# The first level of a chunk inverse, untransposed copy: products X + X Ts in place of transposes

## The chip, the cores and the metric

The kernel runs on one core of a Trainium2 chip. The metric is device time in microseconds for one execution: one layer of a hybrid block (an RWKV-7 recurrence in 8 heads beside sliding-window attention in 8 heads, then a SwiGLU feed-forward layer) for 1024 tokens of width 1024, in float32.

## What is computed

```python
def step(S, inp):                       # one token of the RWKV-7 recurrence, per head
    r_t, w_t, k_t, v_t, kk_t, a_t = inp
    sa = jnp.einsum('bhvk,bhk->bhv', S, -kk_t)
    S = (S * w_t[:, :, None, :]
         + sa[..., None] * (kk_t * a_t)[:, :, None, :]
         + v_t[..., None] * k_t[:, :, None, :])
    return S, jnp.einsum('bhvk,bhk->bhv', S, r_t)
...
o_rwkv = rwkv7_time_mix(p_rwkv, ...)
o_attn = swa_sink_attention(q, k_att, v_att, sinks[l])
x = x + jnp.concatenate([o_rwkv, o_attn], axis=-1) @ w_out[l]
h = rmsnorm(x, norm_ffn_g[l])
gate, up = jnp.split(h @ w_gate_up[l], 2, axis=-1)
x = x + (jax.nn.silu(gate) * up) @ w_down[l]
```

The kernel does not step through tokens. It takes the 1024 tokens in 8 tiles of 128, and within a tile the dependence of a token on the tokens before it is a triangular system with unit diagonal, one 128x128 matrix per head. Its inverse is what this case is about.

## The kernel before

The program has seven stages, one after another on each engine: the input projection, its lanes, attention, the recurrence (the functions named `stage5_...`), the output projection, the feed-forward layer and the last norm. Each engine has its own function per stage, and the functions wait for each other with semaphores. The order on every engine is the order in which the code is written; nothing reorders it.

**The recurrence.** `stage5_tensor` (TensorE), `stage5_vector` (VectorE), `stage5_scalar` (ScalarE), `stage5_sync` (DMA queue) and `stage5_gpsimd` each loop over t = 0 to 7, the tiles of 128 tokens. The 8 heads are worked in two groups g of four, since four 128x128 results fill one PSUM bank of 128x512. `Plan` gives every job (a name, a group, a tile) its bank: `C.claim` waits until the bank's last reader is done, `C.done` marks the last matmul, `C.result` waits for that mark, `C.read` frees the bank after the read, and `C.emptied` waits until that read has ended.

**The inverse of one tile.** VectorE inverts the 16x16 diagonal blocks (`lanes`), and two DMAs bring them as `XT` (the inverse, transposed) into SBUF. Two levels then double the block size, 16 to 32 (level 1) and 32 to 64 (level 2). A level needs both the inverse so far, `X`, and its transpose, `XT`:

- `corners(n, t)`, line 1359: TensorE forms NB times X in the banks `tn0`, `tn1`. VectorE masks the result to the level's corner blocks into `Ts1` or `Ts2` (line 1556).
- `updates(n, t)`, line 1366: TensorE forms Ts times XT in the banks `yn0`, `yn1`, and VectorE adds the changed half of it to `XT` (line 1563), freeing the bank.
- `transposed("x1", g, t)`: after level 1, TensorE waits until the add of group g has ended, transposes its four blocks of the new `XT` (line 1358) into the bank `x10` or `x11`, and ScalarE copies the bank to `X` (`keep_x`, line 1497). Level 2 needs this `X`. At the start of a tile `transposed("xa", ...)` and `keep_x("xa", ...)` do the same with the `XT` that the DMA brought.

**What stands around it.** Between level 1 and level 2 TensorE has two further pieces: `outputs(t - 1)` (line 1385), four transposes of the tile before, from t = 1 on, and `cumulative(pe, t + 2)` (line 1213), eight recorded matmuls for the tile after the next, up to t = 5. On VectorE `normalise(t - 1)` (line 1619) stands behind level 1's mask, and `outputs(t - 1)` (lines 1625 and 1629) behind level 1's adds. In the last tile VectorE also has `mix_low(0)` (line 1266), which prepares the output projection, between `outputs` and level 2's mask. `prepare` (lines 1251 to 1257) and `lanes(t + 1)` follow level 2's adds.

Of the kernel before, what the change touches and what calls it, by code (L numbers as in the profile page):

```python
# [7 lines left out]
ALU = mybir.AluOpType  # L8
# [73 lines left out]
def hybrid_block(nc, x_t, par_in, w_in, w0, w_up, a_up, g_up, sinks, w_out, w_gate_up, w_down, norm_final_g,  # L82
# [10 lines left out]
    def at(name, kb, shape, dt=F32):  # L93
        return nc.alloc_sbuf_tensor_at(name, shape, dt, offset=BASE + int(kb * K))
# [8 lines left out]
    with root:  # L103
# [133 lines left out]
        X, XT = at("X", 112, [P, H, P]), at("XT", 116, [P, H, P])  # L237
# [14 lines left out]
        x1 = at("x1", 72, [P, KD, T])  # L252
# [150 lines left out]
        def row(ap):  # L403
            return ap.rearrange("p a n -> p (a n)")
# [445 lines left out]
        for t in range(-1, NT):  # L850
            n = t + 1
# [331 lines left out]
        C = Plan(order5 + [("ot", NT - 1, 7)])  # L1183
# [47 lines left out]
        def exponentials(act, t, *js):  # L1231
            for j in js:
                b = C.result(act, f"cum{j}", t)
                if t:
                    act.wait_ge(s_prep, 4 * t)
                v = b[:, 0:2 * (P + 1)].rearrange("p (a n) -> p a n", a=2)
                c = slice(2 * j, 2 * j + 2)
                act.activation(ein[:, c, :], v[:, :, :], ACT.Exp, scale=-DECAY)
                act.activation(ecs[:, t, c] if t else ecs0[:, c], v[:, :, P], ACT.Exp, scale=-DECAY)
                if t:  # L1240
                    act.activation(ems[:, t, c], v[:, :, 0], ACT.Exp, scale=DECAY)
                ins = act.activation((einv if t else einv0)[:, c, :], v[:, :, 1:P + 1], ACT.Exp, scale=DECAY)
                C.read(ins, f"cum{j}", t)
# [15 lines left out]
        def mix_high(act, n):  # L1259
            k = MIX_ORDER[n]  # L1260
            act.activation(mhi[:, k, :], mix[:, k, :], ACT.Copy).then_inc(s_m, 1)
# [86 lines left out]
        def stage5_tensor(pe):  # L1348
            def four(b, g, lhs, rhs):
                for j in range(4):  # L1350
                    mm = pe.matmul(b[:, j * P:(j + 1) * P], lhs(4 * g + j), rhs(4 * g + j), start=j == 0, stop=j == 3,  # L1351
                                   skip_group_check=True)
                return mm

            def transposed(job, g, t):
                b = C.claim(pe, f"{job}{g}", t)
                for j in range(4):
                    mm = pe.transpose(b[:, j * P:(j + 1) * P], XT[:, 4 * g + j, :], ident)  # L1358
                C.done(mm, f"{job}{g}", t)
# [7 lines left out]
            def updates(n, t):  # L1367
                m = Ts1 if n == 1 else Ts2
                for g in range(2):
                    C.emptied(pe, f"t{n}{g}", t)  # L1370
                    b = C.claim(pe, f"y{n}{g}", t)
                    C.done(four(b, g, lambda h: m[:, h, :], lambda h: XT[:, h, :]), f"y{n}{g}", t)

            def tokens(t):
                for kind, m in (("bt", ab), ("kt", kT)):
                    b = C.claim(pe, kind, t)
                    for p in range(NP):
                        mm = pe.transpose(b[:, p * P:(p + 1) * P], m[:, p, tok(t)], ident)
                    C.done(mm, kind, t)
# [20 lines left out]
            for t in range(NT):  # L1400
# [4 lines left out]
                for g in range(4):  # L1405
                    C.emptied(pe, f"b{g}", t)
                corners(1, t)
                updates(1, t)
                if t:
                    outputs(t - 1)  # L1410
                for g in range(2):
                    C.emptied(pe, f"y1{g}", t)
                    transposed("x1", g, t)
                if t + 2 < NT:
                    cumulative(pe, t + 2)
                corners(2, t)
                updates(2, t)

                if t:
# [35 lines left out]
                if more:  # L1455
                    b = C.claim(pe, "S", t)
# [35 lines left out]
        def stage5_scalar(act):  # L1492
            low, high = slice(0, HD), slice(HD, P)

            def keep(job, t, dst, rows=slice(0, P)):
                b = C.result(act, job, t)
                C.read(act.activation(dst, b[rows, :], ACT.Copy), job, t)

            def keep_x(job, t):
                for g in range(2):  # L1500
                    keep(f"{job}{g}", t, row(X[:, 4 * g:4 * g + 4, :]))

            def tokens(t):
                keep("bt", t, bt[:, :])
                keep("kt", t, kt_[:, :])

            exponentials(act, 1, 0, 1)
            tokens(0)
            for t in range(NT):
                last = t == NT - 1  # L1510
                keep_x("xa", t)
                if last:
                    mix_high(act, 0)
                keep_x("x1", t)
                if last:
                    mix_high(act, 1)
                if t + 2 < NT:
                    exponentials(act, t + 2, 0, 1)
                if last:
                    mix_high(act, 2)  # L1520
                act.wait_ge(s_r, t + 1)
                act.activation(rs_[low, :], bank[0][low, :], ACT.Copy).then_inc(s_rlow, 1)
                act.wait_ge(s_u, t + 1)
                act.activation(us_[low, :], bank[2][low, :], ACT.Copy).then_inc(s_ulow, 1)
                keep("R", t, rs_[high, :], high)
                keep("U", t, us_[high, :], high)
                if last:
                    mix_high(act, 3)
                if last:
                    for s in range(2):  # L1530
                        OUT.split_hi(act, s, 0, first=True)
                else:
                    C.emptied(act, "S", t)
                    act.wait_ge(s_fac, t + 1)
                    for p in range(NP):
                        ins = act.activation(S[:, p, :], Sn[:, p, :], ACT.Copy, scale=facs[:, t + 1, p:p + 1])
                    ins.then_inc(s_S, 1)
                act.wait_ge(s_oc, t + 1)
                act.activation(osq[:, :, :], oc[:, :, :], ACT.Square).then_inc(s_osq, 1)
                if t + 1 < NT - 1:  # L1540
                    tokens(t + 1)

        def stage5_vector(dve):
            order = Order(dve, "rec_order")

            def halves(ap, n, second):

                w = BLK << (n - 1)
                return ap.rearrange("p h (b n) -> p h b n", n=2 * w)[:, :, :, w * second:w * second + w]
# [9 lines left out]
            def updates(n, t):  # L1559
                for g in range(2):  # L1560
                    b = C.result(dve, f"y{n}{g}", t).rearrange("p (h n) -> p h n", h=4)
                    v = halves(XT[:, 4 * g:4 * g + 4, :], n, 1)
                    C.read(dve.tensor_tensor(v, halves(b, n, 1), v, ALU.add), f"y{n}{g}", t)

            def lanes(t):
# [75 lines left out]
            for t in range(NT):  # L1641
# [22 lines left out]
                if not last:  # L1664
                    b = C.result(dve, "S", t)
# [9 lines left out]
                b = C.result(dve, "O", t)  # L1675
# [829 lines left out]
```

## Time and profile before

| | us |
|---|---|
| median of 3 runs | 1366.65 |
| lowest, highest of the 3 | 1365.69, 1497.57 |
| the profiled execution | 1372.2 |
| its span (first to last recorded instruction) | 1370.1 |
| recurrence, first transposes of t = 0 to the first product of the output projection | 364.65 to 587.82 |

The profile is of one execution. A row of the time line gives the start, the time that the instructions of that row took from the first start to the last end, the engine, the line of the code, the operation with output and inputs, the number of recorded instructions, and in brackets the idle time before it with what ended that idle time. A float32 matmul of the program stands in the trace as two recorded matmuls, a float32 transpose as one. The recorded end of a matmul is modelled and overlaps the next one, so the time that a group takes of TensorE is read from its start to the start of the next group. PE is TensorE, PEld its weight loads, DVE VectorE, ACT ScalarE.

### The profile page before, as it was taken

What the parts mean: (1) busy time and instruction counts of PE and PEld (TensorE: products, weight loads), DVE (VectorE), ACT (ScalarE), POOL (GpSimd) and SP (SyncE); (2) the same over time, 40 slices, a digit from 0 to 9 for tenths busy, and PEclk for the clock granted to TensorE, in tenths of its full rate; (3) what the DMA queues carried; (4) which work ended last, traced back from release to release, by engine and by line L of the source; (5) the groups of instructions that cost most, each with busy time, mean ns of one, the idle gap of its engine ahead of it and who ended that gap; (6) DMA issues with size and microseconds to landing.
All of it is one profiled execution on the core that took longest, in us unless ns stands there. A gap on an engine that the chain in (4) does not pass through costs nothing.

```text
span 1370.1 us, 18353 instructions
## 1 busy us (share of the span) xinstructions
PE 1322.4 (97%) x7169; PEld 1094.5 (80%) x7169; DVE 807.8 (59%) x1212; ACT 466.9 (34%) x864; POOL 169.1 (12%) x144
## 2 busy tenths in 40 slices
PE   7999999898899999999999999999999999999996
PEld 6888887555699899888878888888888887888885
DVE  6644422499677777554476565665656655454545
ACT  6111132577422332333453333333333333021232
POOL 0000000044300000000004223332233100000000
PEclk9999999999999999999999999999999999999999
DMA  5111132200212221333212232222321284241323
GB/s 211 55 46 46 35 104 93 70 1 17 60 52 53 82 66 46 118 128 113 80 64 77 93 92 92 65 75 93 93 93 58 74 298 155 77 154 46 110 91 138
DMA packets 68864, 120.34 MB, mean 88 GB/s; under 512 B 20912, under 2 KB 37296, under 8 KB 68528
## 3 DMA queue, kind: packets, MB, share of 16 engines
q1 hardware_dynamic: 68784, 119.23, 27.0%
q8 instruction: 55, 0.90, 0.3%
q14 instruction: 25, 0.20, 0.0%
HBM read 89.30 MB, written 29.36 MB: 87 GB/s over the span
## 4 chain that ended last, share of the span: by engine, by line
PE 86%; DVE 7%; DMA 2%; ACT 2%; issue 1%; SPq 0%; DVEq 0%; ACTq 0%
PE bank L344 29%; PE bank L2271 27%; PE bank L397 6%; PE bank L1351 4%; PE bank L1225 2%; PE bank L472 2%; PE bank L358 2%; PE bank L1477 1%; PE bank L1435 1%; PE bank L1429 1%; DMA land<-hid_scratch 1%; DVE st L1151 1%; DVE scores L1128 1%; DMA hid_scratch<-hid 1%; PE bank L1358 1%
## 5 line engine op out<-in xcount | busy, mean ns | idle before, releaser
L323 DVE TENSOR_TENSOR ring_wlo<-ring_raw,ring_whi 128x1024 fp32r<-128x1024 f32 (+1 forms) x62 | 73.8, 1190 | 241.1 <-ACT ring_whi L317 240.9
L317 ACT ACTIVATE ring_whi<-ring_raw 128x1024 fp32r<-128x1024 f32 (+1 forms) x62 | 63.7, 1030 | 308.4 <-PE bank L344 232.2
L2271 PE MATMUL bank<-thi,ahi 128*128 128x512 f32 x320 | 124.5, 389 | 0.0
L2271 PE MATMUL bank<-tlo,ahi 128*128 128x512 f32 x320 | 124.5, 389 | 0.0
L2271 PE MATMUL bank<-thi,alo 128*128 128x512 f32 x320 | 124.5, 389 | 0.0
L344 PE MATMUL bank<-hhi,ring_whi 128*128 128x512 f32 x288 | 115.0, 399 | 0.0
L344 PE MATMUL bank<-hlo,ring_whi 128*128 128x512 f32 x288 | 112.8, 392 | 0.0
L344 PE MATMUL bank<-hhi,ring_wlo 128*128 128x512 f32 x288 | 112.8, 392 | 0.0
L2271 PE MATMUL bank<-x1hi,ahi 128*128 128x512 f32 x240 | 93.4, 389 | 0.0
L2271 PE MATMUL bank<-x1lo,ahi 128*128 128x512 f32 x240 | 93.4, 389 | 0.0
L2271 PE MATMUL bank<-x1hi,alo 128*128 128x512 f32 x240 | 93.4, 389 | 0.0
L344 PE MATMUL bank<-x1hi,ring_whi 128*128 128x512 f32 x176 | 68.8, 391 | 1.7 <-DVE ring_wlo L323 1.7
L2271 PEld LDWEIGHTS bank<-thi,alo 128*128 128x128 f32 x320 | 60.1, 188 | 12.5
L2271 PEld LDWEIGHTS bank<-tlo,ahi 128*128 128x128 f32 x320 | 60.1, 188 | 12.5
L2271 PEld LDWEIGHTS bank<-thi,ahi 128*128 128x128 f32 x320 | 60.1, 188 | 12.4
L344 PE MATMUL bank<-mhi,ring_whi 128*128 128x512 f32 x168 | 66.0, 393 | 2.7 <-DVE gat L2225 2.7
L344 PE MATMUL bank<-x1lo,ring_whi 128*128 128x512 f32 x176 | 68.5, 389 | 0.0
L344 PE MATMUL bank<-x1hi,ring_wlo 128*128 128x512 f32 x176 | 68.5, 389 | 0.0
L344 PE MATMUL bank<-mlo,ring_whi 128*128 128x512 f32 x168 | 66.1, 393 | 0.0
L344 PE MATMUL bank<-mhi,ring_wlo 128*128 128x512 f32 x168 | 66.0, 393 | 0.0
L344 PEld LDWEIGHTS bank<-hhi,ring_whi 128*128 128x128 f32 x288 | 54.5, 189 | 12.0 <-issue 1.0
L344 PEld LDWEIGHTS bank<-hlo,ring_whi 128*128 128x128 f32 x288 | 54.4, 189 | 11.9 <-issue 1.0
(314 smaller groups left out, 2863.5 us busy)
## 6 DMA issues: line engine op xcount, KB each, us to landing
ring_raw<-in_w_down SPq DMA_DIRECT2D x24, 512.0 KB, 3.6
hid_scratch<-hid SPq DMA_DIRECT2D x22, 512.0 KB, 6.2
ring_raw<-in_w_in SPq DMA_DIRECT2D x20, 512.0 KB, 3.7
raw_a<-in_w_gate_up SPq DMA_DIRECT2D x20, 512.0 KB, 4.5
raw_b<-in_w_gate_up SPq DMA_DIRECT2D x20, 512.0 KB, 5.1
land<-hid_scratch SPq DMA_DIRECT2D x16, 512.0 KB, 4.1
xin<-in_x_t SPq DMA_DIRECT2D x8, 512.0 KB, 9.6
n_scratch<-NB SPq DMA_DIRECT2D x8, 512.0 KB, 3.2
```

The lines of the kernel that those rows point to most:

```text
L317: act.activation(self.ring.hi[:, s, 0:self.kt, :], self.ring.raw[:, s, 0:self.kt, :], ACT.Copy).then_inc(self.ring.hi_ready, 1)
L323: dve.tensor_tensor(self.ring.lo[:, s, 0:self.kt, :], self.ring.raw[:, s, 0:self.kt, :], self.ring.hi[:, s, 0:self.kt, :].bitcast(F32), AL ...
L344: mm = pe.matmul(o[:, :], wpart[:, s, k, :], apart[:, k, c], start=i == 0, stop=i == n - 1)
L358: mm = pe.matmul(bank[self.J.bank_of[f"{s}{half}"]][:, :], wpart[:, s, ks[n], :], apart[:, ks[n], c], start=n == 0 and i == 0, stop=n == l ...
L397: mm = pe.matmul(o[:, :], wpart[:, s, k, :], apart[:, k, c], start=k == 0 and i == 0, stop=k == self.kt - 1 and i == 2)
L472: mm = pe.matmul(b[:, :], wpart[:, s, k, :], apart[:, k, c], start=k == 0 and i == 0, stop=k == KD - 1 and i == 2)
L1128: ins = dve.scalar_tensor_tensor(sc[:, h0:h0 + 3:2, :], b[:, 0:2 * BAND].rearrange("p (a n) -> p a n", a=2), HD ** -0.5, bias[:, h0:h0 + 3 ...
L1151: order(dve.tensor_reduce(st8[:, 0, :], sc[:, :, :], AX_X, ALU.max))
L1225: mm = pe.matmul(b[e][:, i * 2 * P:(i + 1) * 2 * P].rearrange("p (a n) -> p a n", a=2), src[r, 2 * g + i, tok(t)], rho_alpha(t, r, 2 * g + ...
L1351: mm = pe.matmul(b[:, j * P:(j + 1) * P], lhs(4 * g + j), rhs(4 * g + j), start=j == 0, stop=j == 3, skip_group_check=True)
L1358: mm = pe.transpose(b[:, j * P:(j + 1) * P], XT[:, 4 * g + j, :], ident)
L2271: mm = pe.matmul(b[:, :], w[:, k, :], m[:, k, :], start=opens and k == 0 and i == 0, stop=not (j, n) in parts and k == 3 and i == 2, skip_ ...
```

## The change

Level 1 no longer transposes the updated `XT`. In `updates`, when n is 1, TensorE forms XT times Ts for the same four heads into the bank `x1g`, right behind the product for `y1g`; both use the `XT` from before the update. VectorE adds the changed half of that bank to `X`, ahead of its add to `XT`. The eight transposes of a tile at this place and ScalarE's two copies of a tile are gone. The waits of TensorE for `y10` and `y11` to be emptied stay where they were.

```diff
@@ stage5_tensor, updates
                     C.emptied(pe, f"t{n}{g}", t)
                     b = C.claim(pe, f"y{n}{g}", t)
                     C.done(four(b, g, lambda h: m[:, h, :], lambda h: XT[:, h, :]), f"y{n}{g}", t)
+                    if n == 1:
+                        b = C.claim(pe, f"x1{g}", t)
+                        C.done(four(b, g, lambda h: XT[:, h, :], lambda h: m[:, h, :]), f"x1{g}", t)
@@ stage5_tensor, the loop over t
                     outputs(t - 1)
                 for g in range(2):
                     C.emptied(pe, f"y1{g}", t)
-                    transposed("x1", g, t)
                 if t + 2 < NT:
                     cumulative(pe, t + 2)
                 corners(2, t)
@@ stage5_scalar
-                keep_x("x1", t)
@@ stage5_vector, updates
                     b = C.result(dve, f"y{n}{g}", t).rearrange("p (h n) -> p h n", h=4)
                     v = halves(XT[:, 4 * g:4 * g + 4, :], n, 1)
+                    if n == 1:
+                        bx = C.result(dve, f"x1{g}", t).rearrange("p (h n) -> p h n", h=4)
+                        u = halves(X[:, 4 * g:4 * g + 4, :], n, 0)
+                        C.read(dve.tensor_tensor(u, halves(bx, n, 0), u, ALU.add), f"x1{g}", t)
                     C.read(dve.tensor_tensor(v, halves(b, n, 1), v, ALU.add), f"y{n}{g}", t)
```

TensorE's order in one tile (t = 1), from the first transposes of `XT` to level 2's second product. A row is a group of equal instructions of the program, the number at its end how many. Before:

```order
L1358 MATMUL bank<-cst,XT 128x128 x8
L1351 MATMUL bank<-X,NB_89 128x128 x8
L1351 MATMUL bank<-XT,Ts_90 128x128 x8
L1385 MATMUL bank<-cst,on 128x128 x4
L1358 MATMUL bank<-cst,XT 128x128 x8
L1213 MATMUL bank<-cst,sgt 128x129 x4
L1351 MATMUL bank<-X,NB_89 128x128 x8
L1351 MATMUL bank<-XT,Ts_91 128x128 x8
```

And the same stretch of the changed kernel:

```order
L1358 MATMUL bank<-cst,XT 128x128 x8
L1351 MATMUL bank<-X,NB_89 128x128 x8
L1351 MATMUL bank<-XT,Ts_90 128x128 x4
L1351 MATMUL bank<-Ts_90,XT 128x128 x4
L1351 MATMUL bank<-XT,Ts_90 128x128 x4
L1351 MATMUL bank<-Ts_90,XT 128x128 x4
L1388 MATMUL bank<-cst,on 128x128 x4
L1213 MATMUL bank<-cst,sgt 128x129 x4
L1351 MATMUL bank<-X,NB_89 128x128 x8
L1351 MATMUL bank<-XT,Ts_91 128x128 x8
```

The eight transposes between `on` and `sgt` are gone; eight products (`Ts_90,XT`) stand ahead of `on`, between and behind the products for `y10` and `y11`.

VectorE's order in the same tile, from level 1's mask to level 2's adds. Before:

```order
L1556 TENSOR_TENSOR Ts_90<-bank,cst 128x16x16 x2
L1619 TENSOR_TENSOR on<-oc,sm 128x512
L1563 TENSOR_TENSOR XT<-bank,XT 128x16x16 x2
L1625 TENSOR_TENSOR oc<-bank,arv 128x512
L1629 TENSOR_TENSOR mix<-oc,mix 128x4x128
L1556 TENSOR_TENSOR Ts_91<-bank,cst 128x8x32 x2
L1563 TENSOR_TENSOR XT<-bank,XT 128x8x32 x2
```

The same stretch of the changed kernel:

```order
L1557 TENSOR_TENSOR Ts_90<-bank,cst 128x16x16 x2
L1624 TENSOR_TENSOR on<-oc,sm 128x512
L1567 TENSOR_TENSOR X<-bank,X 128x16x16
L1568 TENSOR_TENSOR XT<-bank,XT 128x16x16
L1567 TENSOR_TENSOR X<-bank,X 128x16x16
L1568 TENSOR_TENSOR XT<-bank,XT 128x16x16
L1630 TENSOR_TENSOR oc<-bank,arv 128x512
L1634 TENSOR_TENSOR mix<-oc,mix 128x4x128
L1557 TENSOR_TENSOR Ts_91<-bank,cst 128x8x32 x2
L1568 TENSOR_TENSOR XT<-bank,XT 128x8x32 x2
```

Two adds to `X` stand ahead of the two adds to `XT`, one for each group of heads.

## Rows read from the trace of the kernel before

**Rows 1.** The page: the span, and TensorE's busy time in it.
```profile
span 1370.1 us, 18353 instructions
PE 1322.4 (97%) x7169; PEld 1094.5 (80%) x7169; DVE 807.8 (59%) x1212; ACT 466.9 (34%) x864; POOL 169.1 (12%) x144
```

**Rows 2.** Busy time by stretch, columns named; one whole tile of the recurrence.
```profile
core 0: us, PE busy (x) PEld busy (x) DVE busy (x) ACT busy (x) POOL busy (x), PEclk, DMA share, GB/s
422.62:450.99 28.37, 28.03 (x261) 26.21 (x261) 21.70 (x48) 8.91 (x24) 1.76 (x3) 1.00 0.23 62
```

**Rows 3.** Waits, 392.9 to 534.6 us (five tiles): total, times, longest.
```profile
PE bank L1351 <- ACT X L1497: 1.7, 5, 0.3
```

**Rows 4.** Time line, tile t = 2, level 1's product to level 2's product.
```profile
424.48 2.00 PE L1351 MATMUL bank<-XT,Ts 128*128 128x128 f32 x16
...
426.32 0.60 PE L1385 MATMUL bank<-cst,on 128*128 128x128 f32 x4
426.52 0.42 DVE L1563 TENSOR_TENSOR XT<-bank,XT 128x256 f32<-128x256 f32 x1 [0.47 <-PE bank L1351]
...
426.75 1.04 PE L1358 MATMUL bank<-cst,XT 128*128 128x128 f32 x8
426.95 0.69 DVE L1625 TENSOR_TENSOR oc<-bank,arv 128x512 f32<-128x512 f32 x1
...
427.63 1.06 PE L1213 MATMUL bank<-cst,sgt 128*128 128x129 f32 x8
427.68 0.69 DVE L1629 TENSOR_TENSOR mix<-oc,mix 128x512 f32<-128x512 f32 x1
...
428.52 1.95 PE L1351 MATMUL bank<-X,NB 128*128 128x128 f32 x16
...
429.62 0.42 DVE L1556 TENSOR_TENSOR Ts<-bank,cst 128x256 f32<-128x256 f32 x1 [1.24 <-PE bank L1351]
...
430.31 1.95 PE L1351 MATMUL bank<-XT,Ts 128*128 128x128 f32 x16
```

**Rows 5.** Time line, tile t = 0, the same place, without `outputs`.
```profile
367.94 1.95 PE L1351 MATMUL bank<-XT,Ts 128*128 128x128 f32 x16
...
369.93 0.42 DVE L1563 TENSOR_TENSOR XT<-bank,XT 128x256 f32<-128x256 f32 x1 [0.47 <-PE bank L1351]
...
370.40 0.42 PEld L1358 LDWEIGHTS bank<-cst,XT 128*128 128x128 f32 x4 [0.32 <-DVE XT L1563]
...
370.90 1.06 PE L1213 MATMUL bank<-cst,sgt 128*128 128x129 f32 x8
```

**Rows 6.** Time line, tile t = 6, without `cumulative`.
```profile
537.95 2.00 PE L1351 MATMUL bank<-XT,Ts 128*128 128x128 f32 x16
...
541.60 2.02 PE L1351 MATMUL bank<-X,NB 128*128 128x128 f32 x16 [0.34 <-ACT X L1497]
```

**Rows 7.** Time line, the last tile, t = 7, level 1 and level 2.
```profile
563.29 3.36 PE L1351 MATMUL bank<-X,NB 128*128 128x128 f32 x16 [0.22 <-ACT X L1497]
...
566.45 2.28 PE L1351 MATMUL bank<-XT,Ts 128*128 128x128 f32 x16
...
570.38 2.02 PE L1351 MATMUL bank<-X,NB 128*128 128x128 f32 x16 [0.34 <-ACT X L1497]
570.54 1.22 DVE L1266 TENSOR_TENSOR mlo<-mix,mhi 128x1024 fp32r<-128x1024 f32 x1
...
571.68 0.42 DVE L1556 TENSOR_TENSOR Ts<-bank,cst 128x256 f32<-128x256 f32 x1
...
572.24 1.96 PE L1351 MATMUL bank<-XT,Ts 128*128 128x128 f32 x16
```

**Rows 8.** Busy time by stretch, columns as in rows 2: PEclk is the mean granted clock.
```profile
361.00:364.60 3.60, 1.88 (x16) 1.62 (x16) 3.29 (x7) 0.00 (x0) 0.00 (x0) 1.00 0.57 183
364.60:1370.10 1005.50, 983.58 (x5394) 837.00 (x5392) 601.95 (x910) 326.18 (x535) 126.99 (x96) 0.99 0.30 95
562.00:592.00 30.00, 28.07 (x208) 26.14 (x208) 14.91 (x23) 11.02 (x15) 2.51 (x3) 0.83 0.30 108
```

## What the change will do to the time

> **What bounds the kernel now.** I read the page first. TensorE is busy for 1322.4 of 1370.1 us [rows 1], so anything that lengthens its own queue shows in the time unless it fills a gap. Next I asked whether the recurrence, where the change lies, is like the whole. One full tile (t = 2) takes 28.37 us and TensorE is busy for 28.03 of them, at full clock; VectorE has 21.70 and ScalarE 8.91 [rows 2]. So TensorE has 0.34 us of gap in a tile. The waits name it: in the five tiles t = 1 to 5 the products of line 1351 waited five times, 0.3 us each, for ScalarE's copy of `X` [rows 3]. With five waits for five tiles that is the copy at the tile's start (`xa`), which stays; the copy after level 1 (`x1`), which the change removes, makes TensorE wait in none of them.
>
> The time line of tile 2 shows why [rows 4]. Level 1's product starts at 424.48, `outputs` at 426.32, the eight `x1` transposes at 426.75, `cumulative` at 427.63, level 2's corners at 428.52. Every group starts while the one before it is still ending: TensorE never stops. VectorE's second add to `XT` (426.52, 0.42 us) is all but over when the transposes start, and ScalarE's copies run under `cumulative`. The chain product, add, transpose, copy that the change shortens is already covered by other work of TensorE.
>
> **What a product and a transpose cost.** Durations overlap, so I take start to start. Sixteen recorded matmuls of level 1 (eight products of the program) take 426.32 - 424.48 = 1.84 us, those of level 2's corners 430.31 - 428.52 = 1.79 us: 0.224 to 0.230 us for one product. Eight transposes take 427.63 - 426.75 = 0.88 us, 0.110 each [rows 4]. The new product has the same shape and types as level 1's, with weight and moving operand exchanged, so 1.79 us for eight, and at most 1.84.
>
> The Trainium skill ("FP8 and Floating Point Precision", "TensorE Precision Notes") says that true fp32 takes four passes through the array. If a transpose were a single pass, four of them for a product would be 0.44 us, and the sum below would be 8 x 8 x (0.44 - 0.224) = 13.8 us larger, some 26 us. The rows show a ratio of two, and the rows decide.
>
> **The change, part by part**, for a tile with all its pieces (t = 1 to 5), counted from the start z of level 1's product:
>
> - Before, `cumulative` starts at z + 3.15 (427.63 - 424.48).
> - After, the products for y10, x10, y11, x11 run without a break: x11 and y11 read only the old `XT` and `Ts`. They end at z + 1.84 + 1.79 = z + 3.63. `outputs` takes 0.43 (426.75 - 426.32) to z + 4.06. If nothing waited, `cumulative` would start there: +0.91 us. This is the plain exchange, 1.79 - 0.88.
> - But the wait for y11 to be emptied stays ahead of `cumulative`, and what empties y11 has moved back. VectorE starts on a bank 0.20 us after TensorE has started the next group (426.32 to 426.52) [rows 4]. It must now have x11, the last of the four, before it adds to `X`, and only then adds to `XT`, which frees y11. It starts at z + 3.83. Two adds of 0.42 follow each other; the second starts some 0.08 before the first ends, as at 570.54 + 1.22 against 571.68 [rows 7]. They end at z + 4.59. From the add's end to the next weight load were 0.05 us in tile 0 (369.93 + 0.42 against 370.40) [rows 5]; I allow 0.10. `cumulative` starts at z + 4.69, so TensorE stands still for 0.63 us. The first group's two adds lie under the products of the second. VectorE's own order, with `X` first in each group, is shown ahead of the rows.
> - Sum: 4.69 - 3.15 = **+1.54 us** a tile, five times.
> - The VectorE adds to `X` (two more of 0.42) delay its `outputs`, which now end at about z + 4.59 + 1.42 - 0.08 = z + 5.93 (the 1.42 is 426.95 to 428.37 [rows 4]). Level 2's first mask is due at z + 4.69 + 0.89 (`cumulative`, 428.52 - 427.63) + 0.90 (half of the corners) + 0.20 = z + 6.68. Hidden, with 0.75 us to spare. VectorE's idle time there, 1.24 us before, is the cover.
> - Removing ScalarE's two copies of a tile gives nothing: nobody waited for them. The DMA queue is not touched; `lanes(t + 1)`, the two DMAs of `XT` and the chain on the state all come after level 2's adds and move with them, so no wait behind them swallows the loss.
>
> Tile 0 has no `outputs`; there the product-to-`cumulative` distance was 370.90 - 367.94 = 2.96 [rows 5]. After: 3.58 + 0.20 + 0.76 + 0.10 = 4.64, **+1.68**.
>
> Tile 6 has no `cumulative`, so here TensorE did wait for the `x1` copy (0.34) [rows 6]: 541.60 - 537.95 = 3.65 before, 4.69 after, **+1.04**.
>
> Tile 7 began at low clock, and from product to corners it was 570.38 - 566.45 = 3.93, so 0.28 above tile 6. With the same surcharge, the corners now start at 566.45 + 4.97 = 571.42. But VectorE has `mix_low(0)` between `outputs` and level 2's mask, and this tile has no `cumulative` to cover it. With tile 2's times: the adds end at 571.32, `outputs` at 572.66, the mask starts 1.14 later (570.54 to 571.68) at 573.80 and ends at 574.22. Level 2's product, 572.24 before [rows 7], starts at 574.3: **+2.06**.
>
> Sum: 1.68 + 5 x 1.54 + 1.04 + 2.06 = **12.5 us**. About 7.3 (8 x 0.91) is more work, the rest is new waiting. The profiled execution, 1372.2, would become 1384.7. It lay 5.5 us above the median of the runs; against the median the forecast is 1366.65 + 12.5 = **1379 us**, 0.9% slower.
>
> **The rivals.**
>
> *The wait costs nothing.* If the adds to `X` and `XT` were quicker or the release earlier than I count, only the exchange stays, with the last tile's queue on VectorE: 7.3 + 1 = 8 us, 1375. For it: each step of the wait is only tenths of a microsecond. Against: the add starts 0.20 us after the next group, and it can't read a bank before its product is done. A lower bound for the whole: no stall at all, 7.3 us, 1374.
>
> *Not slower: the clock pays for it.* From 364.6 to the end the mean granted clock is 0.99; the missing hundredth of 1005.5 us is 10 us of full-speed work, between 5 and 15 by the rounding, and 5.1 of it (17% of 30 us) lies from 562 to 592 us, in the last tile and behind it [rows 8]. That is the half-clock level, 1.2 instead of 2.4 GHz, after TensorE stood and waited. A denser stream of products could shorten those stretches. Taking back the last tile's 5.1 leaves +7.4, 1374; only if more than 12.5 us came back, which is all or more than all that is missing, would the kernel not be slower; at the rounding's far end, 15 us, it would be 1364. Against: the change adds pauses as well as products.
>
> By the Trainium skill ("TensorE: Matmul & The Clock Gate", "Part 4: PE-mode transpose") transposes do not count as TensorE being busy, which is in favour of products in their place. In rows 2 a tile with all its transposes ran at 1.00, so there is nothing to win in seven of the tiles.
>
> *The new pauses cost the clock.* In tile 7 low clock made 16 matmuls of the corners take 3.36 instead of 2.02 us, and with level 1's 0.28 it cost 1.6 us [rows 6, 7]. If the 0.63 us pause did that in seven tiles more: 12.5 + 11 = 23.7, 1390. Against: between 361.0 and 364.6 TensorE was busy for 1.88 of 3.60 us and the clock stayed at 1.00 [rows 8]; a pause of 0.63 in 30 us is far less.
>
> *The exchange doesn't happen.* Excluded by the order of instructions: eight products more and eight transposes fewer stand in each tile.
>
> **How the numbers follow.** The forecast has 0.72. The free wait has 0.13 (1374 to 1376), the clock paying for it 0.05 (1364 to 1374), the clock lost 0.06 (to 1390), and something that I do not see 0.04. The forecast's own spread is the pitch of the new product (1.79 or 1.84, 0.4 us in all), the latencies (0.1 us in 8 tiles, 0.8) and the distance of single executions, of which this case shows 5.5 us between the profile and the median. Together with the free wait that gives 1371 to 1388, which leaves out the low part of the clock's gain and most of its loss. Differences of over 2%, 27 us, are about what a measurement of this kernel tells from no change: only the lost clock with further tiles' trouble reaches that, 0.02; a gain of over 2% has no source, 0.01; within 2%: 0.97.
>
> **What would show it.** Right: in each of tiles 1 to 5 the recurrence is 1.5 us longer (28.37 becomes 29.9); line 1351 has 128 recorded matmuls more, the `x1` transposes 64 fewer; TensorE idles 0.6 us ahead of `cumulative` with the add to `XT` as what ended it; ScalarE has 16 copies fewer; and everything outside the recurrence keeps its length. The step on the wait is wrong if `cumulative` starts straight behind `outputs`. The step on VectorE's cover is wrong if level 2's product waits for the mask in tiles 1 to 5. The last tile is right if level 2's product waits for a mask that stands behind `mix_low(0)`. The whole is wrong if a tile's clock falls below 1.00 or if the sum of the tiles is not the difference of the spans.

## The result, and the profile after

| | before | changed |
|---|---|---|
| median, us (5 runs each) | 1366.37 | 1379.71 |
| lowest, highest | 1363.42, 1497.57 | 1378.59, 1380.38 |
| profiled span, us | 1370.1 | 1378.2 |
| first transposes of t = 0 to first product of the output projection, in the profile | 223.17 | 236.81 |

The ratio is 1.0094, 95% interval 1.0081 to 1.0107, which is 12.8 us (11.1 to 14.6); timed a second time beside the kernel before it was 1.0088 (1.0072 to 1.0104), 12.0 us (9.8 to 14.2). The forecast was 1379 us, 12.5 more than before and within 2%. So it is. (The 1497.57 is one disturbed execution; ratios leave it out.)

The busy time by stretch, the columns as in [rows 2], for the same tile (t = 2, from its first corners to those of the next):

```profile
424.17:454.35 30.18, 29.31 (x269) 27.22 (x269) 22.33 (x50) 7.93 (x22) 1.75 (x3) 1.00 0.22 58
```

The tile grew from 28.37 to 30.18 us. By this view TensorE has 1.28 us more work in it and 0.53 us more idle time (30.18 - 29.31 = 0.87 against 0.34), the clock is 1.00 as before, ScalarE has 0.98 us less. The 1.28 is more than the exchange of transposes for products, 0.91: the busy time also counts the modelled end of `outputs` (0.60 where 0.43 pass to the next start when nothing waits) and 0.20 by which `cumulative` takes longer.

The time line of the changed kernel at the place of [rows 4]:

```profile
426.03 1.11 PE L1351 MATMUL bank<-XT,Ts 128*128 128x128 f32 x8
...
426.97 1.06 PE L1351 MATMUL bank<-Ts,XT 128*128 128x128 f32 x8
427.87 1.06 PE L1351 MATMUL bank<-XT,Ts 128*128 128x128 f32 x8
...
428.76 1.06 PE L1351 MATMUL bank<-Ts,XT 128*128 128x128 f32 x8
...
429.65 0.60 PE L1388 MATMUL bank<-cst,on 128*128 128x128 f32 x4
429.93 0.42 DVE L1567 TENSOR_TENSOR X<-bank,X 128x256 f32<-128x256 f32 x1 [1.03 <-PE bank L1351]
430.27 0.41 DVE L1568 TENSOR_TENSOR XT<-bank,XT 128x256 f32<-128x256 f32 x1
430.60 0.68 DVE L1630 TENSOR_TENSOR oc<-bank,arv 128x512 f32<-128x512 f32 x1
430.79 1.26 PE L1213 MATMUL bank<-cst,sgt 128*128 128x129 f32 x8 [0.53 <-issue]
...
431.88 1.95 PE L1351 MATMUL bank<-X,NB 128*128 128x128 f32 x16
...
432.98 0.42 DVE L1557 TENSOR_TENSOR Ts<-bank,cst 128x256 f32<-128x256 f32 x1 [0.97 <-PE bank L1351]
```

The four product groups run without a break for 3.62 us. VectorE's second pair of adds (429.93 and 430.27) ends at 430.68, and `cumulative` starts 0.11 us later. TensorE stood still for 0.53 us by its own count, which reckons from the modelled end of `outputs`; by the starts it is 430.79 - 429.65 - 0.43 = 0.71 us. The trace names "issue" as what ended it, not VectorE. `cumulative` then takes 431.88 - 430.79 = 1.09 us to the next start instead of 0.89; VectorE's read of `outputs` (430.60, 0.68 us) ends in the middle of it, which will matter below.

The waits of the changed kernel over five tiles, as in [rows 3]:

```profile
PE bank L1213 <- issue: 2.7, 5, 0.5
PE bank L1351 <- ACT X L1499: 1.7, 5, 0.3
```

The old wait at the tile's start is there unchanged, the new one stands beside it, five times in five tiles.

Tile by tile, from one tile's first transposes to the next one's: tile 0 went from 28.17 to 30.00 us (+1.83), tiles 1 to 5 from 28.37 to 30.18 (+1.81 each), tile 6 from 27.24 to 28.33 (+1.09), tile 7, up to the output projection, from 25.93 to 27.60 (+1.67). The sum is 13.6 us; the medians differ by 13.3, and both intervals above hold the 13.6. The two profiled spans differ by only 8.1 us, since the profiled execution of before lost time elsewhere: it was 2.1 us longer ahead of the recurrence and 3.5 us longer behind it. Of the latter 2.7 are a single wait in the feed-forward layer, in the time line of before:

```profile
1143.80 0.60 PE L344 MATMUL bank<-mhi,ring_whi 128*128 128x512 f32 x1 [2.72 <-DVE gat L2225]
```

The changed kernel's profile has no such wait, and nothing in that layer was edited.

Tile 7 has a stretch at low clock, which has to be kept apart from the change. From its first transposes to level 1's product it took 3.26 us in a kernel where the granted clock stayed at 1.00 there (x products first, below); before, it took 4.56 us at 0.70, and in the changed kernel 4.47 us at 0.62 (x products first, before, changed; columns as in [rows 2]):

```profile
572.96:576.22 3.26, 3.04 (x24) 2.69 (x25) 1.46 (x3) 2.60 (x4) 1.83 (x2) 1.00 0.92 392
561.89:566.45 4.56, 4.34 (x25) 3.99 (x25) 1.46 (x3) 2.10 (x3) 1.83 (x2) 0.70 0.63 269
571.77:576.24 4.47, 4.47 (x25) 4.17 (x25) 1.46 (x3) 3.24 (x5) 1.83 (x2) 0.62 0.67 282
```

With the 0.28 us that level 1's product lost before [rows 7], low clock cost 1.58 us before and 1.21 in the changed kernel. At equal clock tile 7 therefore grew by 2.04 us and the recurrence by 14.0.

### The profile page after: what moved, and what is told of

Same layout as the page of the kernel before. It is cut to its first block, busy times and chain, and to the rows that moved or that the text cites. A ratio compares the mean times of both kernels' runs of the same rounds, so it can differ in the third digit from the quotient of the medians.

```text
span 1378.2 us, 18489 instructions
## 1 busy us (share of the span) xinstructions
PE 1328.7 (96%) x7233; PEld 1100.5 (80%) x7233; DVE 813.0 (59%) x1228; ACT 458.7 (33%) x848; POOL 169.2 (12%) x144
## 4 chain that ended last, share of the span: by engine, by line
PE 89%; DVE 7%; issue 2%; ACT 1%; DMA 0%; SPq 0%; DVEq 0%; ACTq 0%
PE bank L344 30%; PE bank L2276 27%; PE bank L397 6%; PE bank L1351 5%; PE bank L358 3%; PE bank L1225 2%; PE bank L472 2%; PE bank L1479 1%; PE bank L1437 1%; PE bank L1431 1%; DVE st L1151 1%; DVE scores L1128 1%; PE bank L1213 1%; PE bank L1449 1%; PE bank L1466 1%
## 5 line engine op out<-in xcount | busy, mean ns | idle before, releaser
L2276 PEld LDWEIGHTS bank<-thi,ahi 128*128 128x128 f32 x320 | 60.1, 188 | 12.5
```

Of the source, the lines that this page charges most:

```text
L2276: mm = pe.matmul(b[:, :], w[:, k, :], m[:, k, :], start=opens and k == 0 and i == 0, stop=not (j, n) in parts and k == 3 and i == 2, skip_ ...
```

## The experiments

Each kernel was timed beside the kernel before on the same chip. The recurrence's length is read from each profile as in the table above. It is one execution, and it includes tile 7, whose stretch at low clock differs by up to 1.6 us between the profiles.

| kernel | ratio to before (95%) | tiles 1 to 5, us each | recurrence, us |
|---|---|---|---|
| changed | 1.0094 (1.0081 to 1.0107) | 30.18 | 236.8 |
| wait ahead of `cumulative` gone | 1.0103 (1.0086 to 1.0120) | 30.18 | 235.9 |
| `outputs` behind the wait | 1.0147 (1.0130 to 1.0165) | 31.03 | 243.1 |
| x products first | 1.0106 (1.0089 to 1.0123) | 30.10 | 235.0 |
| before, eight products a tile added | 1.0103 (1.0082 to 1.0124) | 30.15 | 234.6 |
| wait gone, `cum1` in another bank | 1.0074 (1.0057 to 1.0091) | 29.27 | 231.8 |
| and VectorE reordered in tiles 6, 7 | 1.0044 (1.0027 to 1.0061) | 29.28 | 227.8 |
| x products first, adds early | 1.0072 (1.0049 to 1.0096) | 29.87 | 233.0 |
| reordered, products of 64 columns | 1.0047 (1.0030 to 1.0064) | 29.22 | 228.5 |
| before, gap at the tile's start filled | 0.9978 (0.9967 to 0.9988) | 28.06 | 220.8 |

**The price of the products by itself.** The kernel before, with the change's products added and nothing taken away:

```diff
                     C.emptied(pe, f"y1{g}", t)
+                    four(C.claim(pe, f"x1{g}", t), g, lambda h: XT[:, h, :], lambda h: Ts1[:, h, :])
                     transposed("x1", g, t)
```

> The kernel before, transposes and copies kept, with eight further products a tile of the change's kind (XT times Ts1) ahead of the x1 transposes; their results are overwritten and not used. Theory A (a product costs 0.224 us of TensorE's queue and nothing covers it): each tile 1.79 us longer (28.37 becomes 30.2), sum +14.3 us, 1380.7 us. Rival (four passes against one of a transpose, 0.44 us each): +28 us, 1394 us. Rival (products fill gaps): less than +10 us.

Measured: 1.0103, which is +14.1 us; tiles 1 to 5 are 1.78 us longer (28.37 to 30.15). (The products' results are overwritten by the transposes.) In these tiles the 0.224 us a product hold, nothing covers them, and four times a transpose is excluded. In tiles 0 and 6 the products fell partly into waits that TensorE had there [rows 5] [rows 6], and the tiles grew by 1.50 and 1.32 us only. So the recurrence is 11.4 us longer by this profile, or some 13 with tile 7 taken at equal clock, against the 14.3 expected; the 14.1 of the ratio (11.2 to 16.9) can't tell these apart. The exchange in the change is therefore 1.79 - 0.88 = 0.91 us a tile in tiles 1 to 5, and 0.9 us of its 1.81 must be something else.

**The wait taken away.** `C.claim` of level 2's product for y20 and y21 waits for the same banks, so the order is kept without the explicit wait.

```diff
-                for g in range(2):
-                    C.emptied(pe, f"y1{g}", t)
                 if t + 2 < NT:
                     cumulative(pe, t + 2)
```

> The changed kernel without TensorE's waits for y10 and y11 ahead of cumulative; level 2's own claims of the same banks order XT's add ahead of its read. Theory A (per tile 0.91 us more work and 0.9 us of standing still at that wait, restart included): cumulative follows outputs without a gap, tiles 1 to 5 take 29.3 us instead of 30.18, tile 0 gains 1.2 us, tiles 6 and 7 gain nothing because level 2's mask then waits for VectorE's outputs; sum 5.7 us less than the changed kernel, 1374 us. Theory B (the new products themselves cost 1.8 us a tile and the gap is only where the trace puts it): no change, 1379.7 us.

Measured: 1.0103, no gain against the changed kernel. By the time alone that is theory B. The time line, though, shows a gap that moved:

```profile
430.65 0.60 PE L1388 MATMUL bank<-cst,on 128*128 128x128 f32 x4
430.93 0.42 DVE L1565 TENSOR_TENSOR X<-bank,X 128x256 f32<-128x256 f32 x1 [1.03 <-PE bank L1351]
...
431.08 0.61 PE L1213 MATMUL bank<-cst,sgt 128*128 128x129 f32 x4
431.27 0.41 DVE L1566 TENSOR_TENSOR XT<-bank,XT 128x256 f32<-128x256 f32 x1
431.60 0.68 DVE L1628 TENSOR_TENSOR oc<-bank,arv 128x512 f32<-128x512 f32 x1
...
432.33 0.71 PE L1213 MATMUL bank<-cst,sgt 128*128 128x129 f32 x4 [0.64 <-DVE oc L1628]
...
432.88 1.95 PE L1351 MATMUL bank<-X,NB 128*128 128x128 f32 x16
```

`cumulative` now follows `outputs` at once (430.65 to 431.08), but stops in its middle. Its second half goes to bank 7, where `outputs` has just put its result, and VectorE reads that result (line 1628) only behind the adds. Behind the wait that the prediction named lay a second one of about the same length. Tile 0, which has no `outputs`, did gain what theory A said: 28.79 us instead of 30.00. Tile 7 did not gain, as it said too: TensorE's corners came earlier, but level 2's product still started 7.50 us after level 1's (7.45 in the changed kernel), with VectorE's mask as what ended its wait.

**Both waits taken away.** As above, and:

```diff
-            return [("cum0", t, 1), ("cum1", t, 7)] if t < NT else []
+            return [("cum0", t, 1), ("cum1", t, 7 if t < 2 else 3)] if t < NT else []
```

> As e1_wait_gone, and from tile 2 on cumulative's second half (cum1) goes to bank 3 instead of bank 7, which it shares with outputs. In e1_wait_gone the gap went on inside cumulative, 0.64 us with VectorE's outputs (line 1628) as what ended it. Theory (the next of two waits in a row, the bank of outputs, took the place of the one removed): with another bank cumulative runs through, level 2's corners start 4.95 us after level 1's product instead of 5.86, tiles 1 to 5 take 29.27 us; sum 4.5 us less than e1_wait_gone, 1374 to 1376 us, ratio 1.006 to 1.007. Rival (VectorE is full there, so the wait moves a second time, to level 2's mask behind outputs): tiles stay at 30.1 us, ratio 1.0103.

Measured: 1.0074, just above the 1.006 to 1.007 expected; tiles 29.27 us, as the theory said. The time line of TensorE:

```profile
423.80 1.10 PE L1351 MATMUL bank<-XT,Ts 128*128 128x128 f32 x8
...
427.42 0.60 PE L1388 MATMUL bank<-cst,on 128*128 128x128 f32 x4
427.85 1.06 PE L1213 MATMUL bank<-cst,sgt 128*128 128x129 f32 x8
428.75 1.95 PE L1351 MATMUL bank<-X,NB 128*128 128x128 f32 x16
```

No gap is left, and level 2's corners start 4.95 us after level 1's product, against 5.85 in the changed kernel and 4.04 before. So the 1.81 us of a tile split into 0.91 for the exchange and 0.90 for the waits. Only tile 0 lost by the new bank, 29.20 us against 28.79 with the wait gone: bank 3 is that of `x11`, and without `outputs` in between, `cumulative` takes 1.30 us there instead of 0.90, its second half starting behind VectorE's add to `X` (369.16 to 369.58). VectorE's cover is just used up: its `outputs` ends at 429.77 and level 2's mask starts at 429.84, the moment at which its input is due (428.75 + 0.89 + 0.20).

**The end of the recurrence.** On top of that, VectorE's `outputs` and `mix_low(0)` behind level 2's mask in the last two tiles:

```diff
-                if t:
+                if 0 < t < NT - 2:
                     outputs(t - 1)
-                if last:
-                    mix_low(dve, 0)
                 corners(2, t)
-                if last:
-                    mix_low(dve, 1)
+                if t >= NT - 2:
+                    outputs(t - 1)
                 updates(2, t)
+                if last:
+                    mix_low(dve, 0)
+                    mix_low(dve, 1)
```

> As e5_cum_other_bank, and in the last two tiles VectorE does outputs (and in the last one mix_low(0)) behind level 2's mask instead of ahead of it. Theory (VectorE's queue is what delays level 2's product there): in tile 6 it starts 5.85 us after level 1's product (6.37 in e1_wait_gone), in tile 7 5.9 (7.50); 2 us less than e5_cum_other_bank. What is left against the kernel before is then the exchange of transposes for products alone, 0.3 to 0.9 us a tile, 6 to 7 us: ratio 1.004 to 1.005. Rival (mix_low comes late for the output projection instead): the recurrence ends no earlier than in e5_cum_other_bank.

Measured: 1.0044, 4 us less than the kernel before it. In tile 7:

```profile
565.06 1.06 PE L1351 MATMUL bank<-XT,Ts 128*128 128x128 f32 x8
...
569.07 1.95 PE L1351 MATMUL bank<-X,NB 128*128 128x128 f32 x16
570.86 1.95 PE L1351 MATMUL bank<-XT,Ts 128*128 128x128 f32 x16
```

Level 2's product starts 5.80 us after level 1's (7.86 in the kernel before this one, 0.40 of it low clock), and no `mix_low` came too late: the output projection starts 15.58 us after that product, as in the kernel before. More than the 2 us expected was gained, but part of it is clock. From tile 7's first transposes to level 1's product it took 3.26 us at a granted clock of 1.00, against 4.49 at 0.71 in the kernel without the reordering. Of the 4.0 us between the two profiles 1.23 + 0.40 = 1.6 are thus low clock; the reordering is worth 0.6 us in tile 6 and 1.7 in tile 7. Against the kernel before, the recurrence is then 4.6 us longer by the profiles and 6.2 at equal clock.

**What ends the first wait.** Two kernels. In the first, only TensorE's order is changed, x1g ahead of y1g:

```diff
+                    if n == 1:
+                        b = C.claim(pe, f"x1{g}", t)
+                        C.done(four(b, g, lambda h: XT[:, h, :], lambda h: m[:, h, :]), f"x1{g}", t)
                     b = C.claim(pe, f"y{n}{g}", t)
                     C.done(four(b, g, lambda h: m[:, h, :], lambda h: XT[:, h, :]), f"y{n}{g}", t)
-                    if n == 1:
-                        b = C.claim(pe, f"x1{g}", t)
-                        C.done(four(b, g, lambda h: XT[:, h, :], lambda h: m[:, h, :]), f"x1{g}", t)
```

> The changed kernel with the product for x1g ahead of that for y1g in each group, so that VectorE's add to X of the second group can run under the last product. Theory A (VectorE's two adds in a row end the gap): the gap shrinks by one add, 0.32 to 0.35 us, in all eight tiles, 30.18 becomes 29.85; sum 2.6 us less, 1377 us. Rival (the gap is latency of the semaphores alone, or TensorE's restart): no change, 1379.7 us.

Measured: 1.0106, tiles 30.10 us. Theory A missed by its number, by a mistake in the edit: VectorE's code waits for y before it turns to x, so both adds still stood behind the last product, and nothing was tested but 0.08 us of latency (`cumulative` starts 4.68 us after level 1's product, 4.76 in the changed kernel). The second kernel has VectorE wait for y behind its add to `X`:

```diff
-                    b = C.result(dve, f"y{n}{g}", t).rearrange("p (h n) -> p h n", h=4)
                     v = halves(XT[:, 4 * g:4 * g + 4, :], n, 1)
                     if n == 1:
                         bx = C.result(dve, f"x1{g}", t).rearrange("p (h n) -> p h n", h=4)
                         u = halves(X[:, 4 * g:4 * g + 4, :], n, 0)
                         C.read(dve.tensor_tensor(u, halves(bx, n, 0), u, ALU.add), f"x1{g}", t)
+                    b = C.result(dve, f"y{n}{g}", t).rearrange("p (h n) -> p h n", h=4)
```

> As e3_x_first, and VectorE now waits for the product y only behind its add to X (in e3_x_first it still waited for y first, so that its adds started no earlier). Theory A (VectorE's two adds in a row end the gap): the second group's add to X runs under the last product, cumulative starts 4.35 us after level 1's product instead of 4.76 (4.68 in e3_x_first), tiles 1 to 5 take 29.8 us instead of 30.18; 3 us less than the changed kernel, ratio 1.007 to 1.008. Rival (latency alone): no change against e3_x_first, ratio 1.0106.

Measured: 1.0072, tiles 29.87 us. The time line of tile 2:

```profile
423.63 1.10 PE L1351 MATMUL bank<-Ts,XT 128*128 128x128 f32 x8
...
427.44 0.42 DVE L1568 TENSOR_TENSOR XT<-bank,XT 128x256 f32<-128x256 f32 x1 [0.47 <-PE bank L1351]
...
427.97 1.37 PE L1213 MATMUL bank<-cst,sgt 128*128 128x129 f32 x8
```

`cumulative` starts 4.34 us after level 1's first product (4.68 with the x products first, 4.76 in the changed kernel). VectorE's edit took one add out of the chain, and the 0.34 us is the distance at which two adds follow each other. Of the 0.42 us, 0.12 are given back inside `cumulative`, which takes 1.21 us instead of 1.09: the read that frees bank 7 (427.88 to 428.57) now ends later within it, which fits a longer wait of its second half. VectorE's adds in a row are what ends the wait, although the trace calls it "issue".

**The cover of `outputs`.**

```diff
-                if t:
-                    outputs(t - 1)
                 for g in range(2):
                     C.emptied(pe, f"y1{g}", t)
+                if t:
+                    outputs(t - 1)
```

> The changed kernel with outputs(t - 1) behind the wait for y10 and y11 instead of ahead of it. Theory A (outputs covers 0.43 us of the wait): the gap ahead of outputs grows to about 1 us, tiles 1 to 5 take 30.6 us instead of 30.18, tiles 6 and 7 lose 0.9 to 1.0 us each because VectorE's outputs come later than level 2's mask is due; sum +4.1 us, 1384 us. Theory B (the gap is not that wait): no change, 1379.7 us.

Measured: 1.0147, by the medians 5.5 us more than the changed kernel, in the recurrence 6.3; tiles 31.03 us, 0.85 more, twice the 0.43 expected. The time line:

```profile
428.44 0.63 PE L1388 MATMUL bank<-cst,on 128*128 128x128 f32 x4 [0.97 <-issue]
428.90 0.61 PE L1213 MATMUL bank<-cst,sgt 128*128 128x129 f32 x4
...
429.85 0.71 PE L1213 MATMUL bank<-cst,sgt 128*128 128x129 f32 x4 [0.34 <-DVE oc L1630]
```

The gap ahead of `outputs` is 0.97 us, as expected, and `cumulative` starts 0.45 us later than in the changed kernel. The rest is the shared bank again: `outputs` now stands right ahead of `cumulative`, whose second half waits for VectorE to read it, so that it takes 1.50 us instead of 1.09.

**Half the columns.** VectorE adds only 64 of a product's 128 columns to `X`. On the reordered kernel, only these are formed:

```diff
-                        C.done(four(b, g, lambda h: XT[:, h, :], lambda h: m[:, h, :]), f"x1{g}", t)
+                        for j in range(4):
+                            h = 4 * g + j
+                            mm = pe.matmul(b[:, j * P:(j + 1) * P].rearrange("p (b n) -> p b n", n=32)[:, :, 0:16],
+                                           XT[:, h, :], m[:, h, :].rearrange("p (b n) -> p b n", n=32)[:, :, 0:16],
+                                           start=j == 0, stop=j == 3, skip_group_check=True)
+                        C.done(mm, f"x1{g}", t)
```

> As e6_vector_reordered, and the new products form only the 64 of 128 columns that VectorE adds to X (16 out of every 32). Theory (the pace of these products is set by their weight loads, two of 128 columns each, as the trace's 128x64 products at 0.108 to 0.112 us a recorded matmul suggest): no change, the product group still takes 0.89 us. Rival (pace goes by the moving columns): each group of four products 0.45 us shorter, 0.9 us a tile, 7 us in all, and the kernel would be as fast as before.

Measured: 1.0047 against 1.0044, no gain. The time line of TensorE:

```profile
424.13 1.10 PE L1351 MATMUL bank<-XT,Ts 128*128 128x128 f32 x8
425.06 1.00 PE L1377 MATMUL bank<-Ts,XT 128*128 128x64 f32 x8
425.90 1.11 PE L1351 MATMUL bank<-XT,Ts 128*128 128x128 f32 x8
426.85 1.00 PE L1377 MATMUL bank<-Ts,XT 128*128 128x64 f32 x8
427.69 0.61 PE L1393 MATMUL bank<-cst,on 128*128 128x128 f32 x4
```

A group of 64 columns takes 0.84 us (425.06 to 425.90, 426.85 to 427.69), one of 128 columns took 0.89. The pace of a product this small does not go by its moving columns. The 16-column pieces in which they are taken are not the reason: other products of 64 columns in one piece have the same pace (line 1429 before, 16 recorded matmuls in 1.73 us, 0.108 each, against 0.105 here). That the pace goes by the weight loads fits, but was not shown separately.

**The lesson turned round.** The change shortened a chain that was covered. The gap that is not covered is the 0.34 us at the tile's start [rows 3]. On the kernel before, half of `cumulative` goes there, in bank 3, and the other half stays:

```diff
-            order5 += [("xa0", t, 1), ("xa1", t, 7), ("t10", t, 0), ...
+            order5 += [("xa0", t, 1), ("xa1", t, 7)] + ([("cum1", t + 2, 3)] if t + 2 < NT else []) + [("t10", t, 0), ...
@@ stage5_tensor
                 for g in range(2):
                     transposed("xa", g, t)
+                if t + 2 < NT:
+                    cumulative(pe, t + 2, (1,))
...
-                    cumulative(pe, t + 2)
+                    cumulative(pe, t + 2, (0,))
@@ stage5_scalar
                 keep_x("xa", t)
+                if t + 2 < NT:
+                    exponentials(act, t + 2, 1)
                 keep_x("x1", t)
                 if t + 2 < NT:
-                    exponentials(act, t + 2, 0, 1)
+                    exponentials(act, t + 2, 0)
```

The DMA that refills `sgt` waits for both halves; behind `x11` the plan of the banks keeps `cum0` alone.

> The kernel before, with transposes; cumulative's second half (cum1, tiles 2 on) stands in bank 3 between the first transposes of a tile and level 1's corners, where TensorE waits 0.34 us for ScalarE's copy of X; the first half stays between x1 and level 2. Theory (what the change cost was cover, not chain; the same cover put into a gap gains): the gap ahead of corners closes, the x1 copy stays covered but for about 0.05 us, tiles 0 to 5 take 28.0 us instead of 28.37, sum 2 us less than before, ratio 0.9985. Rival (the copy after level 1 is no longer covered by half of cumulative): the gap comes back there, 0.3 us or more, ratio 1.000 or above. Second rival (the DMA of sgt lands too late for the earlier place): a gap ahead of the moved half.

Measured: 0.9978, interval 0.9967 to 0.9988, 3 us faster than before and clear of 1. The time line of tile 2:

```profile
415.70 1.09 PE L1359 MATMUL bank<-cst,XT 128*128 128x128 f32 x8
...
416.63 0.61 PE L1213 MATMUL bank<-cst,sgt 128*128 128x129 f32 x4
...
417.14 2.02 PE L1352 MATMUL bank<-X,NB 128*128 128x128 f32 x16
...
421.27 1.04 PE L1359 MATMUL bank<-cst,XT 128*128 128x128 f32 x8
...
422.14 0.61 PE L1213 MATMUL bank<-cst,sgt 128*128 128x129 f32 x4
...
422.65 2.02 PE L1352 MATMUL bank<-X,NB 128*128 128x128 f32 x16
```

The moved half, 0.45 us of work, fits in front of the corners without delaying them (1.44 us from the transposes to the corners, 1.43 before). The copy after level 1 is all but covered by the half that stayed: that half takes 0.51 us to the next start instead of 0.45, and the corners behind it 1.86 instead of 1.79. Of the 0.45 us 0.13 are so given back, and the tile takes 28.05 us, 0.31 less. Tiles 0 to 5 together gained 2.0 us, the 2 expected; the ratio's 3 us (1.6 to 4.5) holds that.

**The change once more.**

> The changed kernel once more, beside the kernel before on the same chip and in the same call. Theory (gaps and products as read in its tiles: tile 0 +1.8, tiles 1 to 5 +1.81 each, tile 6 +1.1, tile 7 +1.7, sum 13.6 us): ratio 1.010. If the difference of the profiled spans, 8.1 us, were the true one: 1.006.

Measured: 1.0088, 1379.34 us, interval 1.0072 to 1.0104. It holds the 1.010 of the tiles' sum and leaves out the 1.006 of the two profiled spans, so the tiles' sum is the better account of the change. The measured value lies between the two, and the timing can't tell 13.6 us from the 12.5 of the forecast. The tiles are the same as in the first profile, 30.18 us, and tile 7 takes 27.44 us, with 1.05 of it low clock: at equal clock 26.39, as in the first.

## Why the prediction was right

- *The bound.* TensorE's queue, with a covered chain between the levels: right. The products added to the kernel before cost their full 1.78 us a tile in tiles 1 to 5.
- *The price of the exchange*, 0.91 us: right, and split off by experiment (0.91 us is what remained with both waits gone).
- *The wait for y11*: it is there, in all tiles. It was mis-sized: with z the start of level 1's product, `cumulative` started at z + 4.76 instead of 4.69, since VectorE's add began 0.28 us after the start of the next group, not 0.20. With the wait for one bank ahead of the add (x products first) it was 0.20 again, so the 0.08 is connected with the order of VectorE's two waits. And `cumulative` takes 1.09 us to the next start, not 0.89. In tile 0, which has a pause but no `outputs`, it takes 0.96 (370.57 to 371.53), so some 0.07 is the pace after a pause (with that wait gone the same eight took 0.90, 371.63 to 372.53); the other 0.13 fits the wait of its second half for bank 7, which VectorE frees at 431.28, when that half would be starting. Together 0.27 us a tile, 1.81 for 1.54.
- *The wait as the whole cause*: this was incomplete, and the total did not show it. Had somebody removed that wait on the word of the prediction, nothing would have been gained in tiles 1 to 5, because bank 7, shared by `outputs` and `cumulative`, holds TensorE until the same moment (corners at z + 5.86 instead of 5.85). The prediction had asked what is late next on VectorE (level 2's mask, rightly found covered) but not which banks its late `outputs` holds.
- *VectorE's cover* in tiles 1 to 5: right. Level 2's mask was not late; it waited 0.97 us for TensorE.
- *Tile 7*: the mechanism was right. Level 2's product waited for the mask behind `mix_low(0)`:

```profile
582.09 1.22 DVE L1266 TENSOR_TENSOR mlo<-mix,mhi 128x1024 fp32r<-128x1024 f32 x1
583.22 0.75 DVE L1557 TENSOR_TENSOR Ts<-bank,cst 128x256 f32<-128x256 f32 x2
583.69 1.86 PEld L1351 LDWEIGHTS bank<-XT,Ts 128*128 128x128 f32 x16 [0.92 <-DVE Ts L1557]
583.69 2.05 PE L1351 MATMUL bank<-XT,Ts 128*128 128x128 f32 x16 [0.72 <-DVE Ts L1557]
```

  It was 1.67 us longer, not 2.06. From product to product it took 7.45 instead of 5.79 us, +1.66; the 0.28 us of low clock that the prediction carried over from [rows 7] were not there this time. At equal clock that is 7.45 against 5.51, +1.94, and the whole tile +2.04: the size of the mechanism was right, and what came out smaller is the clock.
- *The sum*: 13.6 us by the tiles for a forecast of 12.5, 13.3 by the medians. The 1.3 us too few in tiles 1 to 5, 0.15 in tile 0 and 0.05 in tile 6 were partly made up by tile 7, that is by low clock that happened to be 0.37 us less. The median hit is thus closer (1379.7 for 1379) than the terms are, and that is luck.
- *The clock* neither paid nor cost in tiles 1 to 5, which stayed at 1.00 with a pause of half a microsecond more in each. In tile 7 it gave back 0.37 us in this pair of profiles; over all the profiles the same stretch took from 3.26 to 4.85 us.
- *The sign that would show it wrong*, a sum of the tiles unlike the difference of the spans, did occur (13.6 against 8.1). It was a bad test, since single executions of one kernel differ by that much; the wait of 2.7 us quoted above is an example.
- *What ended the pause*: the prediction expected VectorE's add to be named; the trace says "issue". That it was the adds is shown by the kernel with the adds early.

## What to carry to other kernels

Before shortening a chain, look whether the engine that bounds the kernel waits for it: here it did not. Two copies that lay hidden under other work were saved, and eight transposes that stood in TensorE's queue were exchanged for products of twice their price in the same queue. An operand made from another engine's adds moves those adds to the end of the whole group, and then every bank that engine reads later is late too; a wait that is removed shows its worth only when the next one, often a shared bank, is known. The same filler work put where TensorE really waits gained 0.2%.

## What the runs showed of the hardware

- A float32 product of 128x128x128 costs TensorE 0.224 us, twice a float32 transpose of the same block (0.110), and forming 64 of its 128 columns saves 0.05 of the 0.89 us of a group of four.
- After a pause TensorE was slower for a moment at full clock: eight recorded matmuls behind one of 0.97 us took 0.96 us instead of 0.89, sixteen in tile 6 took 1.86 instead of 1.79, behind one of 0.53 us (551.47 to 553.33) and, before the change, behind one of 0.34 us (541.60 to 543.46). In these places a pause cost 0.07 us more than its length.
- Low clock in tile 7, after a wait of 1.73 us ahead of it, fell differently from kernel to kernel: level 1's corners there took 3.36 us before, 2.91 in the changed kernel, 3.65 with the wait gone and 2.02 with the x products first (granted clock 1.00), with the same instructions and the same wait ahead. Differences of a single profile's last tile of up to 1.6 us say nothing of an edit.
